# Rotary halves exchanged by DMA, the last expert pass inside the loop, and a reordered softmax in the block solve

## The reference

```python
# first block, forget attention and gated delta rule (4 heads of 128 each)
s = (einsum("bhqd,bhkd->bhqk", q, k) * scale + (c[..., lo:hi, None] - c[..., None, :hi]))
p = softmax(where(mask, s, -inf)); o = einsum("bhqk,bhkd->bhqd", p, v)
sol = triangular_solve(a_mat, rhs, left_side=True, lower=True)      # chunks of 64
# second block, retention (4 heads of 128)
def rotary(x, pos):
    x1, x2 = xf[..., :half], xf[..., half:]
    return concatenate([x1 * cos - x2 * sin, x2 * cos + x1 * sin], axis=-1)
q = rotary(q, pos) * (RET_HEAD_DIM ** -0.5)
k = rotary(k, pos)
# second block, mixture of experts: 64 experts, two per token, then a last rmsnorm
```

## Time and profile before

| what | value |
|---|---|
| median of three runs | 1604.44 us (1604.38 to 1604.44) |
| the profiled execution, its own time | 1605.6 us |
| its span | 1603.8 us |
| mean granted TensorE clock over the span | 0.917 |
| busy share of the span: PE, DVE, ACT | 81%, 38%, 30% |

### The profile page before, as it was taken

The page is one execution under the profiler, slowest core; times in us unless marked ns, Lnnn a source line. Parts: engine busy times, 40 slices in busy tenths (PEclk is TensorE's granted clock), DMA queues, the critical chain, the costliest instruction groups (busy, mean ns, idle before and its releaser), DMA issues.

```text
span 1603.8 us, 32016 instructions
## 1 busy us (share of the span) xinstructions
PE 1292.5 (81%) x14154; PEld 1012.0 (63%) x14154; DVE 611.2 (38%) x986; ACT 474.3 (30%) x767; POOL 0.2 (0%) x4
## 2 busy tenths in 40 slices
PE   9999999999999999998666576575675666657656
PEld 9999999999999999985433333342342333333333
DVE  6967657777977786731101010010010110110001
ACT  6855575566544464521000000000000000000001
POOL 0000000000000000000000000000000000000000
PEclk9999999999999999999888888798797887888879
DMA  8442234454566654799999999999999999999996
GB/s 337 158 155 86 104 132 153 169 178 172 183 240 237 250 179 178 310 339 429 437 434 435 435 432 432 432 432 432 433 432 434 434 433 434 434 435 435 432 431 267
DMA packets 30318, 518.01 MB, mean 323 GB/s; under 512 B 3488, under 2 KB 3616, under 8 KB 5920
## 3 DMA queue, kind: packets, MB, share of 16 engines
q1 hardware_dynamic: 30096, 516.71, 78.4%
q10 hardware_dynamic: 144, 0.17, 0.0%
HBM read 515.81 MB, written 1.05 MB: 322 GB/s over the span
## 4 chain that ended last, share of the span: by engine, by line
PE 53%; DMA 39%; DVE 5%; ACT 2%; issue 1%; SPq 0%; DVEq 0%; ACTq 0%
DMA e_all<-experts 39%; PE psum L359 11%; PE psum L360 11%; PE psum L361 11%; PE psum L991 7%; PE psum L1039 4%; PE psum L1047 2%; DVE w_low L1692 1%; PE psum L595 1%; PE psum L1021 1%; DVE x_yb L2367 1%; ACT x_actT L1605 1%; DVE a_gdn_qk L1741 1%; DMA w_raw<-dense 1%; PE psum L968 0%
## 5 line engine op out<-in xcount | busy, mean ns | idle before, releaser
L991 PE MATMUL psum<-e_all,x_xt 128*32 128x256 f32 x4096 | 292.9, 449 | 222.7 <-DMA e_all<-experts 222.2
L991 PEld LDWEIGHTS psum<-e_all,x_xt 128*32 128x32 f32 x4096 | 144.0, 129 | 361.4 <-DMA e_all<-experts 239.0
L359 PE MATMUL psum<-h_high,w_high 128*128 128x256 f32 x864 | 245.9, 285 | 0.6 <-DVE w_low L1692 0.5
L360 PE MATMUL psum<-h_low,w_high 128*128 128x256 f32 x864 | 242.7, 281 | 0.0
L361 PE MATMUL psum<-h_high,w_low 128*128 128x256 f32 x864 | 242.6, 281 | 0.0
L1692 DVE TENSOR_TENSOR w_low<-w_raw,w_high 128x2048 fp32r<-128x2048 f32 x99 | 226.0, 2289 | 27.9 <-ACT w_high L1131 21.1
L1131 ACT ACTIVATE w_high<-w_raw 128x2048 fp32r<-128x2048 f32 x99 | 189.2, 1914 | 59.7 <-PE psum L361 50.4
L2367 DVE COPY x_yb<-psum 128x256 f32<-128x256 f32 x64 | 27.2, 425 | 429.0 <-PE psum L1039 429.0
L359 PEld LDWEIGHTS psum<-h_high,w_high 128*128 128x128 f32 x864 | 162.7, 188 | 7.6 <-issue 3.8
L360 PEld LDWEIGHTS psum<-h_low,w_high 128*128 128x128 f32 x864 | 162.8, 188 | 0.1
L361 PEld LDWEIGHTS psum<-h_high,w_low 128*128 128x128 f32 x864 | 162.8, 188 | 0.0
(11 more groups left out here) (466 smaller groups left out, 1917.4 us busy)
## 6 DMA issues: line engine op xcount, KB each, us to landing
e_all<-experts SPq DMA_DIRECT2D x55, 6144.0 KB, 45.3
w_raw<-dense SPq DMA_DIRECT2D x100, 1024.0 KB, 4.8
e_all<-experts SPq DMA_DIRECT2D x10, 2048.0 KB, 25.2
e_all<-experts SPq DMA_DIRECT2D x17, 1024.0 KB, 7.0
e_all<-experts SPq DMA_DIRECT2D x2, 4096.0 KB, 20.7
e_all<-experts SPq DMA_DIRECT2D x2, 1536.0 KB, 7.6
e_all<-experts SPq DMA_DIRECT2D x1, 2560.0 KB, 9.0
all_c_late<-c SPq DMA_DIRECT2D x1, 2048.0 KB, 19.6
```

Source lines behind the costliest of these rows:

```text
L359: mm(ps, w[0], src[0], start=start, stop=False, **kw)
L360: mm(ps, w[0], src[1], start=False, stop=False, **kw)
L991: last = mm(half(psum[32 * s:32 * s + 32, GU_BANK[j % 2], 0:256], P), X["xt"][:, k, CAP * j:CAP * (j + 1)], expert_gu(j, k)[:, :, s * P:(s ...
```

## The change

**In the solve.** At levels 0 and 3 DVE now adds the mask to both heads' scores first, takes the maxima of the first head, then (level 3) a low part, then the four subtractions, and only then the maxima of the second head. ACT's order is as it was. At level 2 PE does the two products with the values at the end of the unit, after `solve_tu` and the second half, and DVE takes their results after the four subtractions.

**The rotary step.** The exchange matrix and its matmuls are gone. After each copy of a q or k unit ACT issues two DMAs that copy partitions 64 to 127 of two heads to 0 to 63 of the other tile and the reverse (128 KB each, eight in all). The sign is in the sine table. DVE waits for all four DMAs of q (or k) and multiplies in place; the low part of v21 is made before the rotary step of q, no longer after it. ACT's `keep_sums` of the norm comes before the first copy.

**The last pass.** PE's loop covers it. In all passes there is now a wait ahead of the second half of expert 3's gate and up and of each half of its down product, and ahead of expert 2's down product; SP adds to these semaphores with an instruction of its own where the expert came in one piece. The zero matmuls are done in the first pass only. In the last pass expert 2 arrives in two pieces, too.

```diff
@@ PE, solve levels @@
                 def middle():
-                    for hd in (2 * (lv // 3), 2 * (lv // 3) + 1):
-                        forget[lv % 3](hd)
+                    if lv != 2:
+                        for hd in (2 * (lv // 3), 2 * (lv // 3) + 1):
+                            forget[lv % 3](hd)
                     solve_tu(lv)
                 solve_units[lv](middle)
+                if lv == 2:
+                    forget_pv(0)
+                    forget_pv(1)
@@ PE, retention @@
-            unit("k20", r_gained); rotate("q"); unit("k21", r_gained)
+            unit("k20", r_gained); unit("k21", r_gained)
             pe.wait_ge(sem("input_low"), quarter("n1", 3))
-            unit_tok("v20"); rotate("k"); unit_tok("v21")
+            unit_tok("v20"); unit_tok("v21")
@@ PE, experts @@
-                    if j == 3 and k == DC // 2 and (first or is_last):
-                        add_zeros(24)
-                        pe.wait_ge(sem("gu_loaded3_hi"), 32 if first else 48)
+                    if j == 3 and k == DC // 2:
+                        if first:
+                            add_zeros(24)
+                        pe.wait_ge(sem("gu_loaded3_hi"), (i + 2) * 16)
...
-                    in_halves = j == 3 and (first or is_last)
-                    if in_halves:
+                    if j == 3 and first:
                         add_zeros(16)
...
-                    if first:
-                        pe.wait_ge(sem(f"dn_loaded{j}"), 16 * DN_PIECES[j])
-                    elif in_halves:
-                        pe.wait_ge(sem("dn_loaded3"), 32)
+                    if first or j >= 2:
+                        pe.wait_ge(sem(f"dn_loaded{j}"), (i + DN_PIECES[j]) * 16)
                     for c in range(4):
-                        if in_halves and c == 2:
-                            pe.wait_ge(sem("dn_loaded3_hi"), 16 if first else 32)
+                        if j == 3 and c == 2:
+                            pe.wait_ge(sem("dn_loaded3_hi"), (i + 1) * 16)
...
-            with pe.Fori(1, last_pass) as i:
+            with pe.Fori(1, last_pass + 1) as i:
                 group_pass(i)
-            group_pass(last_pass, is_last=True)
@@ ACT, retention @@
             def turn_raw(nm, u):
...
-                act.sem_inc(sem("raw_qk"), 1)
+                act.dma_start(turned[0:P // 2], raw[P // 2:P]).then_inc(sem(f"turned_{nm}"), 16)
+                act.dma_start(turned[P // 2:P], raw[0:P // 2]).then_inc(sem(f"turned_{nm}"), 16)
             warm(ACT.Sqrt)
+            keep_sums("n1")
             turn_raw("q", 0)
-            keep_sums("n1")
@@ DVE, solve levels @@
                 for hd in pair:
                     if lv % 3 == 0:
-                        fmax(hd)
-                    elif lv % 3 == 2:
+                        fmasked(hd)
+                    elif lv == 5:
                         fout(hd)
+                if lv % 3 == 0:
+                    fmax(pair[0])
                 if 0 < lv < 5:
                     lows(("sv1", "ga00", "ga01", "ga10")[lv - 1])
                 for nm in ("t", "u"):
                     for c in range(2 if nm == "u" or lv < len(LEVELS) - 1 else 0):
                         solve_sub(lv, c, nm)
...
+                if lv % 3 == 0:
+                    fmax(pair[1])
                 for hd in pair:
                     if lv % 3 == 0:
                         fnorm(hd)
+                    elif lv == 2:
+                        fout(hd)
@@ DVE, retention @@
                 for q in range(2):
-                    ps = half(aux.wait(dve, f"rot_{nm}{q}"))
+                    dve.wait_ge(sem(f"turned_{nm}"), 64)
...
-                    V.tensor_tensor(o, ps, sin, ALU.mult)
+                    V.tensor_tensor(o, o, sin, ALU.mult)
...
-                    aux.release(dve, f"rot_{nm}{q}")
...
+            lows("v21")
             rotary("q")
             lows("gc20")
             rotary("k")
@@ SP, experts @@
+            parts_of = {2: ("dn_loaded2",), 3: ("gu_loaded3_hi", "dn_loaded3", "dn_loaded3_hi")}
+            def no_parts(j):
+                for landed in parts_of.get(j, ()):
+                    sp.sem_inc(sem(landed), 16)
...
             def load_expert(i, j):
                 sp.wait_ge(sem("down"), i * GROUP + j)
                 load_part(sp.snap((i % NG) * GROUP + j), 0, EXPERT, E_W[f"all{j}"], f"gu_loaded{j}")
+                no_parts(j)
...
+            for j, parts in ((2, ((0, 2 * SLOT, "gu_loaded2"), (2 * SLOT, SLOT, "dn_loaded2"))),
+                             (3, ((0, SLOT, "gu_loaded3"), (SLOT, SLOT, "gu_loaded3_hi"),
+                                  (2 * SLOT, UNIT, "dn_loaded3"), (2 * SLOT + UNIT, UNIT, "dn_loaded3_hi")))):
```

More of the change, by code:

```diff
@@ L829, in _ @@
             pe.wait_ge(sem("c2_loaded"), 32)
[L830 to L838, removed]
             unit("q20", r_gained, gained_input("n1"), by_chunk=True)
@@ L975, in gather_pair, with gate_up @@
                 gather(2 * q + 1, 4 + q % 2, 1).then_inc(sem("xt_lo" if q < 2 else "xt_hi"), 1)
[L977 removed]
+            def gate_up(i, j, first=False):
                 pe.wait_ge(sem(f"gu_loaded{j}"), 16 * GU_PIECES[j] if first else (i + LOADED_BY[j]) * 16)
@@ L996, in gate_up, with group_pass @@
                 last.then_inc(sem("gate_up"), 1)
-            def group_pass(i, first=False, is_last=False):
+            def group_pass(i, first=False):
                 pe.wait_ge(sem("placed"), i + 1)
@@ L1015, in group_pass @@
                     if j >= 2:
-                        gate_up(i, j, first, is_last)
+                        gate_up(i, j, first)
                     if j == 0:
@@ L1480, in turn_raw @@
                 ps = proj.wait(act, f"{nm}2{u}")
-                link(ac(R[f"{nm}raw"][:, 2 * u:2 * u + 2, :], half(ps), ACT.Copy))
+                raw, turned = (R[k][:, 2 * u:2 * u + 2, :] for k in (f"{nm}raw", nm))
+                link(ac(raw, half(ps), ACT.Copy))
                 proj.release(act, f"{nm}2{u}")
-                act.sem_inc(sem("raw_qk"), 1)
+                act.dma_start(turned[0:P // 2], raw[P // 2:P]).then_inc(sem(f"turned_{nm}"), 16)
+                act.dma_start(turned[P // 2:P], raw[0:P // 2]).then_inc(sem(f"turned_{nm}"), 16)
             warm(ACT.Sqrt)
+            keep_sums("n1")
             turn_raw("q", 0)
-            keep_sums("n1")
             mean_root("n1")
@@ L1878, in softmax_max @@
                     c = slice(lo, lo + w)
-                    last = V.scalar_tensor_tensor(s[:, c], ps[:, c], row(t), mask[:, c], ALU.add, ALU.add)
+                    last = V.scalar_tensor_tensor(buf[:, hd % 2, c], ps[:, c], row(t), mask[:, c], ALU.add, ALU.add)
                 link(last)
                 aux.release(dve, f"{unit}{hd}")
+            def softmax_max(buf, st, pre, hd, spans):
+                st = st[:, 8 * (hd % 2):8 * (hd % 2) + 8]
                 for t, (lo, w) in enumerate(spans):
-                    last = V.reduce_max(st[:, t:t + 1], s[:, lo:lo + w], AX)
+                    last = V.reduce_max(st[:, t:t + 1], buf[:, hd % 2, lo:lo + w], AX)
                 link(last)
@@ L2515, in _ @@
                     load_expert(i, j)
-            for j in range(GROUP - 1):
+            for j in range(2):
                 load_expert(last_pass, j)
-            sp.wait_ge(sem("down"), last_pass * GROUP + 3)
-            e = sp.snap((last_pass % NG) * GROUP + 3)
-            for at, n, landed in ((0, SLOT, "gu_loaded3"), (SLOT, SLOT, "gu_loaded3_hi"), (2 * SLOT, UNIT, "dn_loaded3"),
-                                  (2 * SLOT + UNIT, UNIT, "dn_loaded3_hi")):
-                load_part(e, at, n, E_W["all3"][:, at:at + n], landed)
+            for j, parts in ((2, ((0, 2 * SLOT, "gu_loaded2"), (2 * SLOT, SLOT, "dn_loaded2"))),
+                             (3, ((0, SLOT, "gu_loaded3"), (SLOT, SLOT, "gu_loaded3_hi"),
+                                  (2 * SLOT, UNIT, "dn_loaded3"), (2 * SLOT + UNIT, UNIT, "dn_loaded3_hi")))):
+                sp.wait_ge(sem("down"), last_pass * GROUP + j)
+                e = sp.snap((last_pass % NG) * GROUP + j)
+                for at, n, landed in parts:
+                    load_part(e, at, n, E_W[f"all{j}"][:, at:at + n], landed)
             sp.wait_ge(sem("gate_up"), last_pass * GROUP + (GROUP + 3))
@@ L2570, in constants @@
     hf = P // 2
-    rot = np.zeros((P, P))
-    rot[i[:hf] + hf, i[:hf]] = -1.0
-    rot[i[:hf], i[:hf] + hf] = 1.0
-    put(c2, C2, "rot", rot)
+    sign = np.where(i < hf, -1.0, 1.0)[:, None]
     inv = (np.float32(10000.0) ** (-np.arange(hf, dtype=np.float32) / np.float32(hf))).astype(np.float32)
@@ L2578, in constants @@
     put(c2, C2, "cosq", cos * SCALE)
-    put(c2, C2, "sinq", sin * SCALE)
+    put(c2, C2, "sinq", sign * sin * SCALE)
     put(c2, C2, "cosk", cos)
-    put(c2, C2, "sink", sin)
+    put(c2, C2, "sink", sign * sin)
     for hd in range(H):
```

11 lines of the change are left out of this document (5 added, 6 removed).

## The result

The changed kernel takes 1606.89 us (median of 22 runs, 1603.82 to 1609.49), the kernel before, measured beside it, 1604.60 (22 runs, 1603.63 to 1606.27). The ratio is 1.0015 with a 95% interval of 1.0009 to 1.0021: +2.4 us (2.3 between the medians), where the forecast was -0.5 and 1603.9 us. Its profiled execution took 1605.49 us (span 1603.7), the second shortest of the 22.

What follows compares the result with a forecast made beforehand. PE was taken to bound up to about 700 us, then the expert loads, then PE again at the end. Solve +3.7, rotary -2.3, last pass -1.9 gave -0.5, so 1603.9 us; own range 1601 to 1606.5, whole range 1598.0 to 1607.5.

Steps and rivals of the forecast that it cites:

- the forecast's own stalls: Solve: PE's t of levels 1 and 4 waits 1.4 and 3.0 us for ACT's evacuations of x.
- The rotary term: Rotary step: 3.46 us of PE matmuls saved, less stalls of 0.4 and 0.7; sum -2.3 us.
- the exchanges land in 4 us, hidden: Rotary step: the 128 KB exchanges land in 4 us, within the 7.4 us before the last of k is wanted.
- the exchanges land late: Rival, rotary step: at a 12 us landing k's rotary step comes 4.6 us later, total 1608.5 us; chance 0.09.
- point of decision: Rotary step: the exchange latency, 7.4 us, from which a late landing makes PE wait.
- The solve term: Solve: level 1 costs 1.6 us, level 4 costs 3.2, gains 1.3; carried as +3.7 us with ACT's overlaps.
- The gains up to x of level 4: Solve: 0.9 us of bank waits gone and 0.35 from DVE's earlier low part, about 1.3 us.
- the stalls do not come: Rival, solve: ACT has room, so the solve gives -1.5 us and the total is 1598.7 us; chance 0.21.
- The last pass: Tail: removing the zero matmuls takes 1.97 us off PE, less 0.1 for register waits; sum -1.9 us.
- clock in the tail: Rival, last pass: without the zeros the clock falls, costing 3 us, total 1606.9 us; chance 0.05.
- zeros on waiting time: Rival, last pass: pieces land later than read, so the tail gives 0, total 1605.8 us; chance 0.05.
- One for one: Ahead of the experts: a shift of PE before 690 us shifts the expert loads and the end equally, without slack.

Runs made afterwards that it cites:

- e2_rotary: The kernel before with only the change's edits of the rotary step; 1605.45 us, ratio 1.0004 to the kernel before.
- e4_max_early: The changed kernel with DVE's maxima of the second head directly behind those of the first; 1601.62 us, ratio 0.9982 to the kernel before.
- e7_load_later: e2_rotary with the 1.5 MB expert load issued with v20, no longer with k21; 1602.59 us, ratio 0.9988 to the kernel before.

## Why the prediction was wrong

The path of each delay was right, and the sum came out 2.9 us too low for two reasons, both to the same side: the landing of the exchanges was mis-sized, and the clock behind the forecast's own stalls was put at nothing. The measured 1606.89 lies just above the forecast's own 1601 to 1606.5 and inside the whole range.

**The rotary term failed: -2.3 forecast, -0.4 in the first profile, nothing measurable in time.** From x of level 5 to the first scores the kernel before takes 435.98 us; the changed kernel takes 435.62 and 435.87 in its two profiles, `e2_rotary` 436.03 and `e4_max_early` 436.01. The step that failed is "the exchanges land in 4 us, hidden". The forecast took that from a 512 KB load alone on its queue because the size was nearest. But how long the exchange takes was set by what was in the queues ahead of it, not by its size: 9.33 to 9.78 us behind a 1.5 MB load and a weight load, 4.9 and 5.4 for the same exchange without the first. The forecast even names the early expert load, in the rival "the exchanges land late", and its point of decision held: from 7.4 us on every microsecond is PE's. 9.33 - 7.4 = 1.9 on top of the 0.7 forecast gives 2.6 of wait, and the first profile shows 2.40. The rival was given 0.09 because the transfers are small; it was the true case, at a latency between the forecast's and its own 12 us. `e7_load_later` shows it by taking the load away from ahead of the exchange: 1.9 us back at the first gather (2.9 by the medians), and the wait at 0.80.

**The solve term was too small: +3.7 forecast, +4.6 in the profile, +5.6 timed alone.** The step that failed is one that the forecast does not have: t and u behind its stalls were priced at the full clock. The fall of the clock at level 4 cost 1.29 us, and it came in all three profiles with a wait of 2.8 us there, in some also elsewhere. The forecast asked about the clock in the tail alone. Without that fall the solve's 4.81 is 3.52, for 3.7 forecast. The delays at levels 1 and 4 cost 1.77 and 3.15 us (forecast 1.6 and 3.2), the waits of t 1.52 and 2.79 (forecast 1.4 and 3.0); u waited 0.20 at level 1 as forecast and not at level 4. The chain from the reduction over the exponential, high part and evacuations to t held within 0.1 us at each step of level 3, once the 0.47 us are taken off by which PE came later to that level's scores: the second reduction was forecast at 173.5 and came at 174.03.

The gains up to x of level 4 came to 1.4 us (forecast 1.3), but not as the forecast has them. It counts at level 3 both a bank wait, 0.22 of its 0.9, and 0.35 for DVE starting sooner. There x waits for DVE in both kernels, so the bank wait by itself gives nothing, and what counts is DVE, whose subtractions came 0.31 us sooner after the level's first scores (163.22 to 172.03 for x before, 163.69 to 172.19 now). The wait of 0.55 stays because PE came as much sooner as DVE did. The rival "the stalls do not come" fell: ACT had no room.

The Trainium skill (TensorE: Matmul & The Clock Gate, HAM oscillation) says that waits between short runs of matmuls put the engine back to its low clock. The forecast weighed that rule at the tail, where gaps of 0.35 to 0.55 us left the clock in full; behind single waits of 1.53, 2.66 and 2.79 us the clock did fall, though not in every execution. The section's own example has longer waits between shorter runs, so the traces here agree with its direction and show a case that it does not have.

**The last pass was right:** -1.9 forecast, -1.97 in the second profile and -1.9 for the zeros alone. The rivals "clock in the tail" and "zeros on waiting time" did not come: the window at 1588 us of the changed kernel is at 1.00, and only 0.2 to 0.3 us of the removed time met a wait for data. The room was smaller than the forecast read, which had the last weights landed by 1588.

**One for one was right:** doubled and fourfold matmuls give +3.4 and +11.1 for 3.46 and 10.4 us.

With the two terms as measured in the profile, +4.6 - 0.4 - 1.9 = +2.3, the result. That it fits to a tenth is partly luck: the second profile of the same kernel has a shift of 6.0 at the first gather, 1.55 of it a further fall of the clock.

## What to carry to other kernels

Moving an instruction later on one engine delays on the next engine everything that is written behind its consumer; look there, and move the consumer too (here: 6 us between the same edit with and without it). Price a small DMA by what is issued ahead of it on all queues, and if its latency decides, put large prefetches behind it. A stall on TensorE may cost twice: once as the wait, and once in matmuls at the lower clock behind it, here 1.3 to 1.6 us each time.

## What the runs showed that was not expected

- The clock's fall is not fixed by the length of the wait. Behind 2.8 us it fell in three of three profiles (0.50 to 0.60 granted), behind 2.40 to 2.74 us in one of four, behind 1.5 us in one of four; behind 1.27 us in none. The same kernel showed both at the same place.
- An exchange of 128 KB within SBUF took 9.33, 9.60, 9.76 and 9.78 us on ACT's queue in the four profiles with the early load ahead of it, and 4.9 and 5.4 in the two without. In those four the 1 MB weight load issued between the early load and the exchange landed within 0.7 us of the exchange.
- The issue of such an exchange took ACT 0.47 us for the first of a k pair, which reads the upper half of the partitions, and 0.62 for the second, which reads the lower; whether order or half makes the difference no run shows. A load takes SP 0.33 (one weight load 0.60). With the gaps a pair costs ACT 1.33 us.
